# Wider products in the weighing step of a paged sample attention

## What is computed

```
c_past = cache_kv_latent[i][page_table].reshape(db, past, KV_LORA)
...
s = jnp.concatenate([s_past, s_new], -1) * scale        # (sample, head, t, 4096 + 1)
p = jax.nn.softmax(s, axis=-1)
o_lat = jnp.einsum('bhts,bsc->bthc', p[..., :past], c_past) + jnp.einsum('bhtu,buc->bthc', p[..., past:], c_new)
return jnp.einsum('bthc,chv->bthv', o_lat, w_uv)
```

## Time and profile before

| | us |
|---|---|
| median of 3 runs | 1060.26 |
| lowest, highest | 1059.47, 1062.97 |
| the profiled execution | 1060.0 |
| its span, first to last instruction | 1058.2 |
| TensorE busy | 982.3 |
| VectorE busy | 666.6 |
| ScalarE busy | 386.4 |
| GpSimd busy | 69.0 |

### The profile page before, as it was taken

The page is one execution under the profiler, slowest core; times in us unless marked ns, Lnnn a source line. Parts: engine busy times, 40 slices in busy tenths (PEclk is TensorE's granted clock), DMA queues, the critical chain, the costliest instruction groups (busy, mean ns, idle before and its releaser), DMA issues.

```text
span 1058.2 us, 22630 instructions
## 1 busy us (share of the span) xinstructions
PE 982.3 (93%) x9310; PEld 905.6 (86%) x9310; DVE 666.6 (63%) x1054; ACT 386.4 (37%) x857; POOL 69.0 (7%) x76
## 2 busy tenths in 40 slices
PE   4999999999999996776789999999999999999995
PEld 3899999978988884554468999999999999999995
DVE  7558654775564555666664659698764344777567
ACT  3323434324233242131232223366653113656331
POOL 0000000000000033444400000000000000000000
PEclk9999999999999997789999999999999999999998
DMA  8522456040405166778726673234233343232633
GB/s 248 164 67 74 105 144 155 8 120 22 121 21 146 40 199 249 228 260 269 252 63 223 190 206 88 80 89 112 79 99 90 90 116 83 81 107 61 186 109 129
DMA packets 179382, 136.89 MB, mean 129 GB/s; under 512 B 19220, under 2 KB 163449, under 8 KB 179033
## 3 DMA queue, kind: packets, MB, share of 16 engines
q1 hardware_dynamic: 166442, 93.47, 31.7%
q0 software_dynamic: 10368, 37.75, 10.8%
q10 hardware_dynamic: 2502, 4.68, 1.2%
HBM read 124.17 MB, written 11.80 MB: 128 GB/s over the span
## 4 chain that ended last, share of the span: by engine, by line
PE 75%; DVE 14%; issue 4%; another core or an unknown queue 3%; ACT 2%; DMA 1%; ACTq 0%; DVEq 0%; SPq 0%
PE PS L1990 33%; PE PS L2218 9%; PE PS L2667 8%; PE PS L2729 4%; PE PS L2001 3%; PE PS L2562 3%; PE PS L2390 3%; DVE w_lo L1202 2%; DVE pages_T L1461 2%; PE PS L2255 2%; PE PS L2244 1%; PE PS L2445 1%; PE PS L2232 1%; PE PS L2316 1%
## 5 line engine op out<-in xcount | busy, mean ns | idle before, releaser
L1990 PE MATMUL PS<-x_hi,w_hi 128*128 128x262 f32 (+1 forms) x744 | 163.5, 292 | 2.7 <-DVE x_lo L1249 1.4
L1202 DVE TENSOR_TENSOR w_lo<-w_raw,w_hi 128x2048 fp32r<-128x2048 f32 (+3 forms) x65 | 125.9, 1937 | 60.9 <-ACT w_hi L680 49.3
L1990 PE MATMUL PS<-x_lo,w_hi 128*128 128x262 f32 (+1 forms) x744 | 159.5, 286 | 0.0
L1990 PE MATMUL PS<-x_hi,w_lo 128*128 128x262 f32 (+1 forms) x744 | 159.1, 285 | 0.0
L680 ACT ACTIVATE w_hi<-w_raw 128x2048 fp32r<-128x2048 f32 (+3 forms) x59 | 94.5, 1602 | 147.0 <-PE PS L1990 88.5
L1990 PEld LDWEIGHTS PS<-x_hi,w_hi 128*128 128x128 f32 x744 | 120.1, 190 | 6.0 <-issue 2.4
L1990 PEld LDWEIGHTS PS<-x_lo,w_hi 128*128 128x128 f32 x744 | 119.7, 190 | 0.0
L1990 PEld LDWEIGHTS PS<-x_hi,w_lo 128*128 128x128 f32 x744 | 119.5, 190 | 0.0
L2218 PE MATMUL PS<-x_hi,w_hi 128*128 128x262 f32 (+1 forms) x256 | 78.0, 305 | 0.0
L2390 PE MATMUL PS<-pages_T,q_blocks 128*32 128x128 f32 x1024 | 49.7, 304 | 26.7 <-issue 16.0
L631 POOL DMA_INDIRECT pages_c<-in_cache_kv_latent_dram,page_rows x48 | 46.4, 966 | 426.5 <-DVE w_uk_T L1508 371.1
(11 more groups left out here) (380 smaller groups left out, 2305.6 us busy)
## 6 DMA issues: line engine op xcount, KB each, us to landing
w_raw<-in_w_ffn_in_dram SPq DMA_DIRECT2D x44, 512.0 KB, 4.8
w_raw<-in_w_in_dram SPq DMA_DIRECT2D x37, 512.0 KB, 7.0
w_raw<-in_w_ffn_out_dram SPq DMA_DIRECT2D x28, 320.0 KB, 3.8
w_raw<-in_w_o_dram SPq DMA_DIRECT2D x12, 512.0 KB, 6.5
w_raw<-in_w_ffn_out_dram SPq DMA_DIRECT2D x16, 384.0 KB, 4.0
gate_scratch<-gate_out ACTq DMA_DIRECT2D x8, 524.0 KB
gates<-gate_scratch SPq DMA_DIRECT2D x8, 524.0 KB, 8.5
x_T_scratch<-x_sum_T SPq DMA_DIRECT2D x1, 2144.0 KB, 7.6
```

The source lines that it names most:

```text
L1202: V.tensor_tensor(WL[:, par, 0:nk], RAW[:, par, 0:nk], WH[:, par, 0:nk].bitcast(F32), ALU.subtract).then_inc(s_wsplit, 1)
L1990: last = T.matmul(PS[:, bank, 0:n], w[:, par, k, m * P:(m + 1) * P], x[:, k0 + k, half * n:(half + 1) * n], start=start and k == 0 and w i ...
```

## The change

`weigh_chunk` makes two products for each chunk instead of four. Each takes two neighbouring rows of the page, 512 columns moving, and fills a whole PSUM bank in width. The stationary operand is as before, 32 columns for four neighbouring k. Of the result rows 0 to 7 with columns 0 to 255 (row r) and rows 8 to 15 with columns 256 to 511 (row r + 1) are wanted. Even chunks write partitions 0 to 63, odd chunks 64 to 127, so the first chunk of each kind starts the sum. `outputs_back` copies 128 x 512, `out_parts` has twice the width, and `latent_turn` makes four products: for each half of the latent one with the old selection matrix on the first 256 columns and one with a new one (columns 82 to 89 of the small constants, which grow from 82 to 90) on the second 256.

```diff
-    m = np.zeros((P, 82), f32)
+    m = np.zeros((P, 90), f32)
...
             m[32 * g + h, 58 + h] = 1.0
+            m[32 * g + HEADS + h, 82 + h] = 1.0
...
-            ("score_parts", [P, 2, P]), ("out_parts", [P, KVL]), ("q_blocks", [P, 2, 9, 32]),
+            ("score_parts", [P, 2, P]), ("out_parts", [P, 2 * KVL]), ("q_blocks", [P, 2, 9, 32]),
...
-                nc.scalar.activation(OPART[:], PS[:, pv_bank(b), 256:256 + KVL], ACT.Copy).then_inc(S["o_parts"], 1)
+                nc.scalar.activation(OPART[:], PS[:, pv_bank(b), :], ACT.Copy).then_inc(S["o_parts"], 1)
...
                 for ct in range(2):
-                    last = T.matmul(PS[:, pv_bank(b), 144 + 8 * ct:152 + 8 * ct], OPART[:, ct * P:(ct + 1) * P],
-                                    SMALL[:, 58:58 + HEADS], start=True, stop=True)
+                    for s, col in enumerate((58, 82)):
+                        last = T.matmul(PS[:, pv_bank(b), 144 + 8 * ct:152 + 8 * ct],
+                                        OPART[:, KVL * s + ct * P:KVL * s + (ct + 1) * P],
+                                        SMALL[:, col:col + HEADS], start=s == 0, stop=s == 1)
...
-                for r in range(4):
-                    k = 4 * c + r
-                    last = T.matmul(PS[32 * r:32 * r + 32, pv_bank(b), 256:256 + KVL],
-                                    PB[:, par, k:k + 4, :].rearrange("p k h -> p (k h)"), page(b, c)[:, r, :],
-                                    start=c == 0, stop=False, skip_group_check=True)
+                for r in range(0, 4, 2):
+                    k, g = 4 * c + r, 64 * (c % 2) + 16 * r
+                    last = T.matmul(PS[g:g + 32, pv_bank(b), :], PB[:, par, k:k + 4, :].rearrange("p k h -> p (k h)"),
+                                    page(b, c)[:, r:r + 2, :].rearrange("p r c -> p (r c)"),
+                                    start=c < 2, stop=False, skip_group_check=True)
                 last.then_inc(S["pv_chunk"], 1)
                 if c == NCH - 1:
-                    T.matmul(PS[0:HEADS, pv_bank(b), 256:256 + KVL], PB[0:DEC, par, 32, :], CTX[0:DEC, :], start=False,
+                    T.matmul(PS[0:HEADS, pv_bank(b), 0:KVL], PB[0:DEC, par, 32, :], CTX[0:DEC, :], start=False,
                              stop=True, skip_group_check=True).then_inc(S["pv_full"], 1)
```

## The result

The changed kernel takes 1067.64 us (median of 6 runs, 1065.66 to 1072.33) where the kernel before takes 1061.77 us (6 runs, 1059.47 to 1064.62). The ratio is 1.0061, with a 95% interval of 1.0033 to 1.0090: slower, by 5.9 us. The forecast was 1060.9 us, range 1056.3 to 1064.0.

A forecast was written before the change was run, and what follows sets the result against it. In the gather loop, readers of TensorE's results were taken to start with GpSimd's gather issues. Latent turns after it add 0.14 + 0.47 = +0.6 us to 1060.0; 0.26 us to the median gives 1060.9 us, range 1056.3 to 1064.0.

The forecast's parts named there:

- Step 1, weighing products: Weighing: 256 records of 512 columns instead of 512 of 256 stream the same columns; -0.1 to +0.1 us per sample, taken 0.
- Step 2, column groups: A chunk touches two column groups instead of four; claimed no cost, also for chunks 2 and 3 standing alone; taken 0.
- The named other bound: Chunk 3 lasts 0.86 instead of 0.43 us, its signal to GpSimd 0.43 us late in five samples: 2.2 us.
- The mark that I set for it: Sign of a column-group cost: GpSimd's third-chunk issue more than 1.3 us after the second half's scores.
- The rival's chance of 0.11: Rival that chunk 3 is slower in two column groups: 2.2 us, 1063.1; above 1064 if dense runs lose too; chance 0.11.
- Step 3, latent turns: Latent turns have four more records, +0.47 us per sample; taken 0 in five gather-loop samples, 0.14 and 0.47 us after.
- the other bound of the prediction: Five latent turns in the gather loop cost 5 x 0.47 = 2.4 us, or 5 x 0.75 = 3.75 us, instead of 0.
- The +0.61 us behind the loop: Latent turns of samples 6 and 7, after the gather loop: 0.14 + 0.47 us coming through to the end.
- Step 4, the copy: ScalarE's copy to SBUF takes 589 ns, +0.21 us, hidden in the loop and by 0.36 us of cover at the end.
- The rival "fewer records": Gather loop: fewer TensorE records make L1564 less late, 0.8 us in each of five samples, 4 us faster: 1056.9; chance 0.26.
- The rival "turns in the loop": Gather loop: the latent turns' records, not the gather issue, set L1576's start; 2.4 to 3.75 us, 1063.3 to 1064.7; chance 0.13.
- The clock: Rival in the gather loop: one stretch more or less at 1.2 instead of 2.4 GHz moves the end about 1 us.

The follow-up runs named there:

- b_half: Kernel before with half the weighing products (even chunks rows 0 and 2, odd chunks rows 1 and 3, 256 columns each): 0.9987 of the kernel before.
- b_two_groups_3: Kernel before, still four products of 256 columns per chunk, but every chunk on two column groups: 1.0058 of the kernel before, which takes 1057.68 us on that chip.
- before_again: The kernel before, unchanged, run again for its trace on a chip of the faster kind: 1024.37 us.
- a_join_2: Changed kernel with chunk 3 weighed directly behind chunk 2, before the second half of the scores, on a slower chip: 1.0126 of the kernel before.
- b_c3_two_groups_2: Kernel before with only chunk 3 on two column groups instead of four, on a slower chip: 1.0032 of the kernel before.
- a_c3_four_3: Changed kernel with chunk 3 again weighed by four products of 256 columns in four column groups, on a slower chip: 1.0045 of the kernel before.
- run 512: Not a follow-up run: the words are "dense run" and "512-column records", weighing records back to back; 32 take 3.64 us, 64 of 256 columns 3.66 us.

## Why the prediction was wrong

**What bounds the kernel.** Right that the readers' starts go with GpSimd's issues; wrong that their grouping stays as it is. I took it from four samples that all had the same grouping, three and two. After the change the grouping is five, the turns (by readings of the maxima) last 19.3 to 20.3 us behind the first, and the sixth turn 19.3 instead of 13.5 us; the last issue falls at 539.5 instead of 532.7 us.

**Step 1, weighing products, 0: right.** 32 records in 3.64 us against 64 in 3.66 us.

**Step 2, column groups, taken 0: the step that failed.** The choice between "any four records run abreast" and "the two records of a product follow each other in their group" went the wrong way: the lone chunk's signal is 0.43 us later. The named other bound had the size of the delay right and its price too low: 0.43 us in each of five samples, 2.2 us. The mark that I set for it, an issue more than 1.3 us behind the scores, was no clean one, since two samples of the kernel before meet it at the lower clock. Measured on late chips, with this edit alone in the kernel before: 3.4 us for chunk 3 alone (1.8 to 4.9 by the interval), 6.1 us for all chunks (3.8 to 8.5). The rule of the Trainium skill that I set beside it (TensorEngine Tiling, "Key Properties" and "Theoretical Speedup": tiles work independently) agrees with that: 32 records of even and odd chunks together keep the pace (3.64 us), and a lone chunk's signal comes as late as half the rate would make it. The rival's chance of 0.11 was too small for a rule that a page states and no row contradicted.

**Step 3, latent turns: the size right, the cover not shown.** Eight records take 1.06 us in the loop against 0.61 us for four, +0.45, and 0.99 against 0.51 us at the end, +0.48. That is at a granted clock of 1.00; in three of the five turns of the changed kernel the clock is 0.50 and they take 1.88 us (455.73, 515.66 and 536.03), in one 1.56. The kernel before has 0.61 in all five, so by my estimate the five turns last 8.3 instead of 3.1 us, 5.2 us more, above the other bound of the prediction. On a prompt chip four turns in the kernel before cost nothing (0.9999), and half the turns in the changed kernel gain nothing (0.9950 against 0.9936). On a late chip it wasn't tried alone, and "I take 0" rested on a reader that would go on starting with the gather issue, which it no longer does: a part of the changed kernel's loss, at most the whole, may be theirs. The +0.61 us behind the loop isn't seen: that stretch is 0.6 us shorter.

**Step 4, the copy: right.** 0.60 us against 0.589, ready at 574.35 and taken at 574.47: 0.12 us of cover is left.

**The rival "fewer records"**: its mark came true, L1565 begins 0.1 us after L2418 (it was about 2 us), but not its gain: the lateness came back behind L2422, 4.0 us. Its mechanism is borne out as far as the maxima go (12 punctual signals against 16 late ones, split by the number of records); its price was the maxima's alone. `b_half` (0.9987) shows no gain from fewer records on a late chip. On prompt chips the changed kernel is faster by 0.6%, from another place, the "issue" gaps.

**The rival "turns in the loop"**: its mark came true. L1577 begins at 496.27, 0.04 us after the end of L2435 and 2.87 us after the last gather issue, and so it is, within 0.04 us, in all five samples: the eight records and not the issue set its start. This is the rival that the experiments left untested on a late chip, see step 3. **The clock**: one stretch more or less was priced at 1 us; the clock falls in every turn (0.82 against 0.93 in the window). `b_two_groups_3` has its loss at 0.95, so that loss isn't the clock's; a share of the changed kernel's may be.

**What stays open**: why TensorE's signals and work come late beside gather issues on some chips; by what mechanism fewer records make the maxima punctual; on what path the column groups cost 6.1 us in `b_two_groups_3`; how the loss of the changed kernel divides over the groups, the longer latent turns, the fewer records and the lower clock, since their effects go through the grouping of the issues and don't add up. By the traces, the punctual maxima let VectorE transpose two pages earlier, GpSimd's next two issues follow without the pause, and the run of five then covers the spread maxima; no run moved the issues alone.

## What to carry to other kernels

Before work is regrouped onto fewer column groups, look for products that stand alone between two waits: in the dense run here the pace stayed, and the lone chunk's signal came 0.43 us later, as if it took twice its time. Where readers' starts follow another engine's activity and not their producer's end, don't hold that pattern fixed when you cost an edit: say what a shift of 0.4 us would regroup, and give the range for it. A change below 1% in such a loop should be timed on more than one chip; here its sign depends on it.

## What the runs showed of the hardware

- The same kernel takes 1057 to 1062 us on some chips and 1022 to 1026 us on others. The difference lies in the stretch with indirect gathers: loop turns of 17.5 us against 13.2 (423.0 to 502.1 us in six turns of `before_again`), at clocks of 0.93 and 1.00 and transfers of 260 and 313 GB/s; from the last reading of the maxima to the end it is 505.8 and 507.5 us.
- On the slower ones most TensorE signals given in a run of gather issues are seen 0.1 to 1.3 us after the run's end, up to 4.6 us late (`b_half`). Not all: the maxima of the kernels with four records in most chunks are given inside a run and seen within 0.2 us. Signals of VectorE and ScalarE that I looked at inside a run took 0.06 us (485.63 to 485.69 in `a_join_2`) and 0.05 us (492.27 to 492.32 in the kernel before).
- There TensorE works in portions of about four or five records with gaps of 0.3 to 0.5 us (changed kernel, 490.40 to 494.38) or 0.8 to 1.0 us (`a_join_2`), during the run and 1 to 2 us after it.
- A lone chunk on two column groups gives its signal 0.43 us later than on four, at the full clock: 1.63 or 1.64 us behind the scores in 13 samples of three kernels (changed, `b_two_groups_3`, `b_c3_two_groups_2`) against 1.20 or 1.21 in seven of two (before, `a_c3_four_3`); the first sample of the kernel before and of `b_c3_two_groups_2` has less, 0.87 and 0.95. That is what half the rate gives by the estimate of step 2 (0.86 instead of 0.43 us).
- The eight records of the four float32 products of a latent turn (L2435, 8 columns each) take 1.06 us at a granted clock of 1.00 and 1.88 us at 0.50.
- In a dense run 512-column records cost the same as twice as many of 256 columns: 32 take 3.64 us, 64 take 3.66 us.
